# Two orders in the down product's block rows: ScalarE's rounding of the second row's units, and SP's loads of block weights

## The reference

```python
def swiglu(x, w_gu, w_down):
    gate, up = jnp.split(x @ w_gu, 2, axis=-1)
    return (jax.nn.silu(gate) * up) @ w_down
...
        x = x + 0.5 * rmsnorm(swiglu(rmsnorm(x, n[0]), w1_gu[l], w1_down[l]), n[1])
        m, S_a, S_r = mixer(rmsnorm(x, n[2]), pos, w_in[l], ...)
        x = x + rmsnorm(m, n[3])
        x = x + 0.5 * rmsnorm(swiglu(rmsnorm(x, n[4]), w2_gu[l], w2_down[l]), n[5])
```

## Time and profile before

| | |
|---|---|
| time, median of 3 runs | 2180.26 us (2179.63 to 2182.09) |
| profiled execution, its own time | 2179.85 us |
| its span, first to last instruction | 2178.0 us |
| TensorE busy | 2106.5 us, 97% |
| VectorE, ScalarE, GpSimd busy | 67%, 46%, 38% |
| mean granted TensorE clock | 0.987 of full speed |
| HBM traffic over the span | 102 GB/s |

### The profile page before, as it was taken

How to read it: one execution, slowest core, us unless ns; L and a number is a source line. 1 busy time by engine, 2 the same in 40 slices (tenths; PEclk the granted TensorE clock), 3 DMA queues, 4 the chain that set the end, 5 groups by cost and what they waited for, 6 DMA issues and landing times.

```text
span 2178.0 us, 42928 instructions
## 1 busy us (share of the span) xinstructions
PE 2106.5 (97%) x16987; PEld 2079.0 (95%) x16987; DVE 1459.2 (67%) x2271; ACT 991.6 (46%) x1851; POOL 824.8 (38%) x708
## 2 busy tenths in 40 slices
PE   8999989999999999989999998999999999999798
PEld 8999989999989999989999998999999899999798
DVE  6888732587367888863288887317863788888432
ACT  4555433442354555533355554335424454555333
POOL 3433333443315533333443333343432345333332
PEclk9999999999999999999999999999999999999999
DMA  5334523322234233443323444342221343343422
GB/s 150 88 103 127 175 74 112 94 78 73 66 95 137 77 88 113 129 144 93 112 70 88 118 128 140 92 127 70 79 69 58 103 129 90 102 126 109 144 74 85
DMA packets 380713, 224.69 MB, mean 103 GB/s; under 512 B 10356, under 2 KB 371624, under 8 KB 379240
## 3 DMA queue, kind: packets, MB, share of 16 engines
q1 hardware_dynamic: 363568, 213.20, 33.4%
q10 hardware_dynamic: 16952, 8.81, 1.4%
HBM read 200.41 MB, written 21.56 MB: 102 GB/s over the span
## 4 chain that ended last, share of the span: by engine, by line
PE 81%; DVE 8%; issue 6%; ACT 2%; POOL 1%; DMA 0%; DVEq 0%; POOLq 0%; SPq 0%; ACTq 0%
PE ps L817 37%; PE ps L878 22%; PE ps L993 11%; PE ps L1010 4%; PE ps L1092 1%; POOL w_lo L737 1%; DVE x L2323 1%; DVE w_lo L2063 1%; DVE y L2317 1%; DVE tmp L2079 1%; DVE xs_lo L1957 0%; DVE ps L2049 0%; DVE ps L2057 0%; DVE ps L2052 0%; ACT w_hi L1527 0%
## 5 line engine op out<-in xcount | busy, mean ns | idle before, releaser
L737 POOL TENSOR_TENSOR w_lo<-raw,w_hi 128x512 fp32r<-128x512 f32 (+2 forms) x452 | 522.3, 1167 | 744.0 <-ACT w_hi L1460 743.8
L1460 ACT ACTIVATE w_hi<-raw 128x512 fp32r<-128x512 f32 (+2 forms) x452 | 230.8, 527 | 415.8 <-PE ps L817 227.1
L878 PE MATMUL ps<-xb,w_hi 128*128 128x272 f32 x1872 | 355.9, 288 | 0.0
L817 PE MATMUL ps<-xs_hi,w_hi 128*128 128x288 f32 (+1 forms) x1568 | 344.8, 291 | 4.4 <-DVE xs_lo L1957 4.2
L817 PE MATMUL ps<-xs_hi,w_lo 128*128 128x288 f32 (+1 forms) x1568 | 340.6, 288 | 0.0
L817 PE MATMUL ps<-xs_lo,w_hi 128*128 128x288 f32 (+1 forms) x1568 | 339.6, 288 | 0.0
L878 PEld LDWEIGHTS ps<-xb,w_hi 128*128 128x128 f32 x1872 | 294.5, 188 | 0.9 <-DVE late_lo L2063 0.9
L878 PE MATMUL ps<-xb,w_lo 128*128 128x272 f32 x944 | 272.3, 288 | 0.0
L817 PEld LDWEIGHTS ps<-xs_hi,w_hi 128*128 128x128 f32 x1568 | 257.4, 189 | 11.0 <-DVE xs_lo L1957 6.2
L817 PEld LDWEIGHTS ps<-xs_lo,w_hi 128*128 128x128 f32 x1568 | 257.9, 189 | 0.2
L817 PEld LDWEIGHTS ps<-xs_hi,w_lo 128*128 128x128 f32 x1568 | 256.6, 188 | 0.0
(11 more groups left out here) (349 smaller groups left out, 4628.5 us busy)
## 6 DMA issues: line engine op xcount, KB each, us to landing
raw<-in_w_gu_dram SPq DMA_DIRECT2D x176, 512.0 KB, 4.2
raw<-in_w_down_dram SPq DMA_DIRECT2D x132, 256.0 KB, 3.1
raw<-in_w_in_dram SPq DMA_DIRECT2D x56, 512.0 KB, 3.8
h_away<-low_away SPq DMA_DIRECT2D x44, 272.0 KB, 4.6
h_lo<-h_away SPq DMA_DIRECT2D x8, 1088.0 KB, 8.5
raw<-in_w_out_dram SPq DMA_DIRECT2D x16, 512.0 KB, 3.6
raw<-in_w_down_dram SPq DMA_DIRECT2D x16, 384.0 KB, 3.7
raw<-in_w_down_dram SPq DMA_DIRECT2D x16, 320.0 KB, 4.3
```

Source lines behind the costliest of these rows:

```text
L737: pool.tensor_tensor(lo, raw[:, u, k0:k0 + n, :], hi.bitcast(F32), ALU.subtract)\
L817: mm = pe.matmul(bank_part(bank, a), w, v[:, k, TOK[a]], start=(start and n == 0), stop=(stop and n == 2))
L878: mm = pe.matmul(ps[:, j, 0:TH], w[j][:, k, :], xb_part(c_, part, n)[:, k, :], start=(k == 0 and m == 0), stop=(k == KH - 1 and m == 2))
L1460: act.activation(hi, raw[:, u, k0:k0 + n, :], ACT.Copy).then_inc(hi_split, 1)
```

## The change

It has two parts and a third that goes with them. SP issues the three fetches of h's low parts ahead of the three loads of block weights. ScalarE no longer rounds row 0's unit 3 at the end of `up`, but behind input block 0; it rounds row 1's unit 0 behind input block 1 and row 1's unit 1 behind input block 2, ahead of the block weights; row 1's units 2 and 3 stay behind the block weights. The table load and `a_w` come behind `block_rows`.

```diff
@@ SP, ffn
-                down_blocks(l, f, 0, w_down)
                 for part in range(3):
                     fetch(l, f, part)
+                down_blocks(l, f, 0, w_down)
@@ ScalarE, up
                 pair_high(l, f, NPAIR - 1)
-                for u in (2, 3):
-                    split_high(l * GROUPS + DOWN[f], u, BLOCK_KT)
+                split_high(l * GROUPS + DOWN[f], 2, BLOCK_KT)
@@ ScalarE
+            def input_high(l, f, kp):
+
+                act.wait_ge(dt_step.sem, dt_step.at(l, (f * KPAIRS + kp) * 5 + 4))
+                act.activation(dt_part(kp, 0), dt_source(kp), ACT.Copy).then_inc(dt_high.sem, 1)
+
             def block_rows(l, q, g0):
 
                 f = q // 2
-                for kp in range(KPAIRS):
-                    act.wait_ge(dt_step.sem, dt_step.at(l, (f * KPAIRS + kp) * 5 + 4))
-                    act.activation(dt_part(kp, 0), dt_source(kp), ACT.Copy).then_inc(dt_high.sem, 1)
+                input_high(l, f, 0)
+                split_high(g0, 3, BLOCK_KT)
+                input_high(l, f, 1)
+                split_high(g0 + 1, 0, BLOCK_KT)
+                input_high(l, f, 2)
+                split_high(g0 + 1, 1, BLOCK_KT)
                 for r in range(ROW_PAIRS):
...
                     for j in DOWN_HIGHS[0:NTERM - 1]:
                         down_term_high(l, f, r, j)
-                    for u in range(UNITS):
+                    for u in range(UNITS) if r else (2, 3):
                         split_high(g0 + 2 * r + 1, u, BLOCK_KT)
@@ ScalarE, post_norm
                 if q != 1:
+                    block_rows(l, q, g0)
                     act.preload_act_table_set(LN_EXP)
                 if q == 0:
                     act.wait_ge(a_loaded, l * 16 + 16)
                     act.activation(a_w[:, :, 0:GR], a_raw[:, :, :], ACT.Copy).then_inc(a_high.sem, 1)
-                if q != 1:
-                    block_rows(l, q, g0)
```

## The result

The kernel with the change takes 2140.71 us in the median of 6 runs (2140.44 to 2141.17); the kernel before takes 2180.7 (2179.63 to 2182.09). The ratio is 0.9817, 95% interval [0.9804, 0.9829]: some 40 us faster. The forecast was 2144, with 2135 to 2157 as its range. The profiled execution took 2140.78 us.

The account below looks back on a forecast made before the run. TensorE was busy for 97% of the span, so only its idle time and clock could be won. 149.4 - 4 x (27.8 + 0.4) = 36.6 us off 2179.85 gave 2143.2, with 0.4 for the median 2144; range 2135 to 2157.

Parts of the forecast that it names:

- The walk: First down stage followed with the durations of its rows: stalls sum to 4.45 us, a stage takes 27.8 us.
- the measure of rows 2: First to last start of rows 0 and 1's third products: 149.4 us over four down stages, 23.3 each at full clock.
- the lower bound of 2134: Bound of the walk in a down stage: VectorE and GpSimd not meeting at all, 2.3 us shorter (25.5).
- the upper bound of the meeting: Down stage: each meeting costs VectorE and GpSimd the 0.74 of a whole half unit, 1.6 us more (29.4).
- The clock: Low clock (1.2 GHz) behind stalls in the down stages: 0.4 us a stage, bounds 0 and 2 x 1.8.
- The rival that let it fall in each stage: The clock falls in every down stage and isn't swallowed: 9 us more, 2153; chance 12%.
- the slower one: TensorE could stay at 1.2 GHz from row 1's start to the end of the block terms: 2213; chance 3%.
- the 14 us: Loss in the four down stages before the change, at a low clock behind eight idle stretches, 1.8 us each.
- The fetch: First fetch of h's low parts, row 0: lands 1.9 to 3.6 us earlier, wait of 2.70 us falls to 0.
- The waits for `w_lo`: TensorE's stalls for GpSimd's low parts ahead of row 1's units 0, 1 and 2: 1.95, 1.6 and 0.9 us.
- The meeting of VectorE and GpSimd: Half units split beside VectorE's blocks and sums: +0.55 us on VectorE each, GpSimd's half unit 1.2 to 1.5.
- the cover of 0.6: Row 1's first unit, issued some 1.5 us later by SP, lands at 271.9 and is wanted at 272.5.

Follow-up runs that it names:

- experiment 2: The changed kernel with SP's old order (block weights ahead of the fetches): 2142.63 us, ratio 0.9825 to the kernel before.
- experiment 3: The changed kernel with the table load and the rounding of a_w back ahead of the block rows: 2140.43 us.
- experiment 6: The changed kernel, but ScalarE rounds row 1's unit 1 ahead of input block 2 instead of behind it: 2147.77 us.
- experiment 10: experiment 5 plus Experiment 8, with row 1's unit 0 loaded before the block weights and rounded before block 1, unit 1 before block 2: 2140.91 us.
- experiment 5: The changed kernel, but VectorE takes the low parts of the input blocks behind block 2 and the sums: 2135.37 us.
- Experiment 8: The changed kernel, but SP issues the first two fetches ahead of the up stage's last weight load and the last part sent away: 2140.41 us.
- experiment 4: The changed kernel, but SP holds the second fetch back until the last part of h_lo is on its way out: 2140.67 us.
- experiment 11: experiment 10 with row 1's unit 2 also rounded ahead of ScalarE's block weights: 2134.86 us.

## Why the prediction was right, and where its steps were off

**The mechanism.** ScalarE's order held row 1, and the order alone (experiment 2) gives 39 us, of 40 with both parts. Within that order the table load's place is worth nothing (experiment 3); how much is due to row 0's unit 3 behind block 0 and how much to row 1's units ahead of the block weights, no run tells apart. Behind the change the chain is the one walked through: block from VectorE, round, split on GpSimd, and row 1 waits in short pieces for `w_lo`. The walk had block 2 ready at 276.8, or 277.3 with the half microsecond by which this stage now starts later; it was ready at 276.89. It had the block terms at 289.1 (289.6); they started at 289.04.

**The size.** 36.6 us were predicted and the span lost 39.1. By the measure of rows 2 a stage was to take 27.8 + 0.4 and took 27.5. So the error is 4 x 0.3 from the walk and 4 x 0.4 from the clock. Two slips in the text's sums changed nothing here: the range from 2135 does not take in the lower bound of 2134, and the upper bound of the meeting, 1.6 us a stage, is 6.4 us in all, where the sentence on the rule in full has some 5.

**The clock.** I took 0.4 us a stage; nothing was lost. The waits were 1.5 at most, and behind none of them did the clock fall. The rival that let it fall in each stage, and the slower one, did not come. Experiments 6 and 10, with waits of 2.7 and 2.3, show that it was near: there the clock fell again, in two and in three of four stages. The reading of the kernel before was off in a detail: not eight idle stretches had a low clock behind them but seven. In the second stage TensorE waited longest but one for the fetch, and the next full microsecond ran at 1.00:

```profile
953.27 0.49 PE L993 MATMUL ps<-h_hi,w_hi 128*128 128x272 f32 x2 [3.06 <-DMA h_lo<-h_away]
```

```profile
954.00:955.00 1.00, 1.00 (x11) 1.00 1.02 427
```

Nor are the 14 us all due to the clock: by the 0.25 us that a short wait costs beyond what is listed (below), I estimate 2 of them for the eight waits. The length of a wait alone did not decide whether the clock fell, and that no wait of the new kernel was followed by a fall was in part luck: the forecast had waits of up to 1.95, and 1.99 had been enough in the third stage.

**The fetch.** This step was wrong. I took 0 us of wait and gave 0.8 as the most; measured were 1.00, 0.82, 0.77 and 1.49 (0.2 to 1.3 in experiments 3, 5 and 6, with the same order on SP). On the stage's own clock the first fetch landed 1.7 us earlier than before (266.2 + 0.5 - 265.0), where I had given 1.9 as the least and 3.6 as the most. In the other stages it landed 2.2, 1.2 and 2.3 earlier. The least was the 768 KB no longer ahead of it, and over the four stages that is what came (1.9 on the mean); what I had added on top, the earlier issue, brought nothing. Row 0's last weights and the part sent away, issued just before, are still ahead of it in a stream that moves 281 to 339 GB/s at first, not 397. Experiment 8 agrees: issued ahead of these two, the first fetch lands after 5.0 to 5.8 us, not 7.1 to 7.4. That they are the whole reason isn't shown. The second fetch close behind is not it: held back, it changed nothing that can be told from the scatter (experiment 4). The error cost nothing, since row 1's chain absorbed it (experiments 2 and 8).

**The waits for `w_lo`.** Predicted 1.95, 1.6 and 0.9; measured 0.52, 1.16 and 0.49. Of the difference of 2.3, 1.0 is the fetch wait, which the walk had put at 0 and which stands in their place; another 1.0 is what TensorE loses at each of the four waits beyond the idle time that the view lists, 0.24 to 0.27 us each (from 273.88 to 274.81, for one, two pairs start 0.93 apart in place of 0.25, and the next follows after 0.34; 0.52 is listed). The walk had counted that as wait. In all a stage lost 27.5 - 23.3 = 4.2 us, against 4.45.

**The meeting of VectorE and GpSimd.** I took +0.55 for VectorE's operation; it was +0.40 to +0.43 in nearly all cases (0.44 to 0.84 up to 0.87). Here the walk was right in kind and too dear by a quarter: I had taken the one meeting that cost most. The trace of the kernel before had two others on VectorE, at +0.43 and +0.41:

```profile
263.32 1.71 DVE L2199 TENSOR_TENSOR tmp<-h_hi,h_lo 128x1088 f32<-128x1088 f32 x1
265.07 0.85 DVE L2204 TENSOR_TENSOR tmp<-tmp 128x272 f32<-128x272 f32 x1
```

By the rule of the Trainium skill ("SBUF — State Buffer", Who interferes with whom) that was weighed there (exclusion for the whole instruction, +0.74) the stages would have been longer still; the trace does not bear that out for VectorE. GpSimd's half unit of 0.74 becomes 1.2 on the mean in block 2 (2.35 for two), but only 0.8 and 0.9 in block 1 and in the sums (1.65 and 1.80 for two), where I had written 1.2 to 1.5.

**The order on SP.** The blocks were to leave at 260.3 to 261.3, and the first left at 261.08, 0.3 later on the stage's own clock; row 1's first unit left at 262.92, on that clock 2.0 us later than before where 1.5 was said. It landed at 272.7, and ScalarE took it at 272.82. So the cover of 0.6 was nearly used up, but no more. Only in the fourth stage does the view list a wait of ScalarE for it (its timeline there), and TensorE lost nothing, as the 27.5 of that stage shows:

```profile
2003.26 0.73 ACT L1460 ACTIVATE w_hi<-raw 128x256 fp32r<-128x256 f32 x2 [0.48 <-DMA raw<-in_w_down_dram]
```

**The table load.** Predicted as free with 0.25 us left in its gap; 0.21 were left. That it was worth nothing to move it (experiment 3), the prediction did not say: it had the removal in the walk.

What stays open: why the clock fell behind waits of 1.99, 2.32 and 2.72 us and not behind others of 2.16, 2.32, 2.71 and 3.06. No run here tells that apart.

## What to carry to other kernels

When several short waits hang on one chain of engines, total them per stage and ask what sets the last of them: removing the first ones (the fetch here) only lengthens the next, and two edits that each look worth their wait don't add up. Test a new order by moving the work of the engine that paces the chain (two operations of 1.28 us moved on VectorE gave 5 us over four stages), not that of the one that TensorE is seen to wait for. And prefer a few short waits to one long one: with the waits gathered ahead of one unit (experiment 6) this kernel was 7 us slower in the median. Its profile, of the fastest run, shows 3.2 us of that as later work and 2.9 behind two falls of the clock.

## What the runs showed of the hardware that was not expected

- Waits of TensorE of up to 1.6 us in this code (1.62 in experiment 11) were not followed by a lower granted clock. Waits of 1.99, 2.70 and 3.80 (before), 2.91 and 4.29 (experiment 2), 2.72 (experiment 6, twice) and 2.32 to 2.34 us (experiment 10, three times) were, at 0.50. Waits of 3.06 (before), 2.16 (experiment 2, twice), 2.71 and 2.73 (experiment 6) and 2.32 (experiment 10) were not.
- TensorE loses some 0.25 us at each short wait beyond the idle time that the profile lists (3.17 us listed and 4.2 lost in a stage of the full change).
- A transfer of 1088 KB on SP's queue was not measurably slowed by another of the same size issued close behind it: 6.9 to 7.4 us with the second 0.5 us behind (first stage of the full change and of experiments 3, 5 and 6), 7.1 with it 2.8 us behind.
- The table load took 1.28 us, and the next activation started 0.02 us behind it (354.63 and 355.93).
